# A hybrid decode step on one core: other slots for the pieces of the decode attention, and the first page gathers ahead of four memsets

## What is computed

```python
kc, vc = compress(rows[:, :, 0]), compress(rows[:, :, 1])   # every 16 tokens: an MLP over 32 tokens
o_cmp, p = cmp_attention(q, kc, vc)                         # softmax over 255 compressed keys
sel = top_k(select_blocks(p), 16)                           # 16 blocks of 64 tokens per kv head
o_slc = attention(q, k[sel], v[sel])                        # "chosen" keys and values
o_win = attention(q, window of the newest 512 tokens)       # "newest" keys and values
y = layernorm(alpha * x + (gated sum of all) @ w_out)
```

## Time and profile before

| | us |
|---|---|
| median of 3 runs (range) | 2114.49 (2113.04 to 2121.23) |
| the profiled execution's own time | 2107.58 |
| its span in the trace | 2105.8 |
| TensorE busy | 1971.9 (94%) |
| VectorE, ScalarE, GpSimd busy | 882.5, 735.3, 565.1 |
| loop of 384 slots, first product to the end of the last | about 1165.5 to 1839.2 |
| output projection, up to the last product | about 1839.2 to 2072 |

### The profile page before, as it was taken

How to read it: one execution, slowest core, us unless ns; L and a number is a source line. 1 busy time by engine, 2 the same in 40 slices (tenths; PEclk the granted TensorE clock), 3 DMA queues, 4 the chain that set the end, 5 groups by cost and what they waited for, 6 DMA issues and landing times. The chain is left out here.

```text
span 2105.8 us, 25188 instructions
## 1 busy us (share of the span) xinstructions
PE 1971.9 (94%) x9303; PEld 1356.8 (64%) x9303; DVE 882.5 (42%) x1781; ACT 735.3 (35%) x1345; POOL 565.1 (27%) x585
## 2 busy tenths in 40 slices
PE   8999999999999999999996898888888888899997
PEld 7888888888888887777774454444444444444442
DVE  0354545454531014444445355454554545511127
ACT  0231133213310003223323665666566665510013
POOL 0000000000002003343345476656466565030000
PEclk9999999999999999999998999999999999999999
DMA  5222222222222321111114555547374563563224
GB/s 199 89 80 91 91 71 80 91 91 71 80 82 102 100 95 48 61 41 41 41 41 140 170 160 171 168 156 218 107 211 143 176 214 111 196 241 142 80 80 161
DMA packets 76486, 248.95 MB, mean 118 GB/s; under 512 B 11764, under 2 KB 35520, under 8 KB 62176
## 3 DMA queue, kind: packets, MB, share of 16 engines
q1 hardware_dynamic: 46312, 148.04, 20.4%
q0 software_dynamic: 28800, 95.45, 15.0%
q10 hardware_dynamic: 1280, 4.23, 0.5%
HBM read 225.17 MB, written 22.49 MB: 118 GB/s over the span
## 5 line engine op out<-in xcount | busy, mean ns | idle before, releaser
L292 PE MATMUL pj<-xT,strips 128*128 128x260 f32 x2368 | 533.2, 384 | 6.3 <-DMA xT<-d_xT 6.3
L292 PEld LDWEIGHTS pj<-xT,strips 128*128 128x128 f32 x2368 | 446.4, 191 | 72.3 <-issue 6.2
L1869 ACT ACTIVATE big<-dtb 64x512 f32<-64x512 f32 x512 | 302.9, 592 | 164.0 <-PE dtb L1601 152.3
L792 PE MATMUL pj<-xT,strips 128*128 128x260 f32 x1216 | 291.0, 387 | 0.0
L1624 PE MATMUL dpH<-big,w 128*128 128x512 f32 x512 | 274.3, 621 | 0.9 <-DVE hs L1992 0.9
L792 PEld LDWEIGHTS pj<-xT,strips 128*128 128x128 f32 x1216 | 222.0, 190 | 59.1 <-issue 29.6
L1975 DVE TENSOR_TENSOR big<-big 128x512 f32<-128x512 f32 x128 | 88.1, 689 | 217.9 <-ACT big L1869 217.9
L1018 POOL MEMSET kbd<- 128x128 f32 x1 | 0.2, 204 | 635.9 <-POOLq L126 635.9
L1044 POOL TENSOR_SCALAR old<-old,rd 128x128 f32<-128x128 f32 (+3 forms) x116 | 122.0, 1066 | 166.8 <-DVE rd L1153 166.8
L1601 PEld LDWEIGHTS dtb<-const,xT 128*128 128x128 f32 x512 | 66.3, 150 | 127.8 <-issue 86.9
L1567 POOL DMA_INDIRECT KV<-d_cache,gi x104 | 102.4, 985 | 169.4 <-DVE gi L2111 140.1
(11 more groups left out here) (312 smaller groups left out, 2345.4 us busy)
## 6 DMA issues: line engine op xcount, KB each, us to landing
strips<-d_w_in SPq DMA_DIRECT2D x60, 1024.0 KB, 5.1
xT<-d_w_out SPq DMA_DIRECT2D x16, 1024.0 KB, 7.7
d_win_sample<-Wt SPq DMA_DIRECT2D x8, 1024.0 KB, 7.3
Xr<-d_w_out SPq DMA_DIRECT2D x8, 1024.0 KB, 8.6
Wt<-d_win SPq DMA_DIRECT2D x8, 896.0 KB
oT<-d_cache SPq DMA_DIRECT2D x84, 80.0 KB
xT<-d_xT SPq DMA_DIRECT2D x8, 520.0 KB, 9.8
Sold<-d_state SPq DMA_DIRECT2D x8, 512.0 KB, 5.2
```

Of the source, the lines that this page charges most:

```text
L292: mm = nc.tensor.matmul(pj[b][:, a, 0:TH], w[b][:, k, :], xT[:, k, a * TH:(a + 1) * TH], start=(k == 0), stop=(k == KT - 1))
L792: mm = nc.tensor.matmul(bank(s)[:, n, 0:TH], w[s % 2][:, k, :], xT[:, k, n * TH:(n + 1) * TH], start=(k == 0), stop=(k == KT - 1))
L1869: ins = A(dst[:, :, :, hd], tb[bank][hd * DH:(hd + 1) * DH].rearrange("p (j h n) -> p j h n", j=2, h=2), ACT.Copy)
```

## The change

New slots for 17 of the 36 entries of `AT` (`LAST` stays), and on GpSimd the first four gathers stand ahead of the memsets.

```diff
         AT = {
-            "queries": 19, ("second", 0): 27, ("second", 1): 29, "scores": 31, "weights": 35, "sums": 37,
-            "first": 38, "turned": 40, "values": 41, "slots": 42, "bases": 43, "rows": 48,
-            ("second", 2): 53, "fetch0": 54, ("second", 3): 55, "keys0": 58, "mix": 59, "fetch1": 61, "acc": 62,
-            "keys1": 64, "fetch2": 73, "keys2": 76, "fetch3": 80, "keys3": 82,
-            "SCORES": 87, "SCALE": 92, "TURNED": 94, "VALUES": 97, "NEWEST0": 99, "NEWEST1": 100,
-            "WSCORES": 105, "WSCALE": 108, "WTURNED": 111, "WVALUES": 113, "SUM": 114, "DONE": 118,
+            "queries": 19, ("second", 0): 26, ("second", 1): 29, "scores": 31, "weights": 35, "sums": 37,
+            "first": 38, "values": 41, "slots": 42, "bases": 43, "turned": 46, "rows": 48,
+            ("second", 2): 53, "fetch0": 54, ("second", 3): 56, "keys0": 57, "mix": 59, "fetch1": 61, "acc": 62,
+            "keys1": 63, "fetch2": 73, "keys2": 75, "fetch3": 78, "keys3": 81,
+            "SCORES": 87, "SCALE": 92, "NEWEST0": 93, "NEWEST1": 99, "TURNED": 100, "VALUES": 103,
+            "WSCORES": 106, "WSCALE": 108, "WTURNED": 112, "WVALUES": 114, "SUM": 117, "DONE": 124,
         }
@@ gpsimd
-            for n in range(2):
-                nc.gpsimd.memset(qbd[n][:], 0.0).then_inc(init, 1)
-            nc.gpsimd.memset(pn[:], 0.0).then_inc(init, 1)
-            nc.gpsimd.memset(sc[:], FORCED).then_inc(init, 1)
-
             def rows(b, q, par):
...
-            for q in range(4):
+            rows(0, 0, 0)
+            for n in range(2):
+                nc.gpsimd.memset(qbd[n][:], 0.0).then_inc(init, 1)
+            nc.gpsimd.memset(pn[:], 0.0).then_inc(init, 1)
+            nc.gpsimd.memset(sc[:], FORCED).then_inc(init, 1)
+            for q in range(1, 4):
                 rows(0, q, 0)
```

## The result

The changed kernel takes **2066.54 us** (median of 4 runs, 2063.09 to 2067.57) against 2113.76 (median of 4, 2111.83 to 2121.23) for the kernel before: ratio 0.9767, 95% interval 0.9741 to 0.9794. The forecast was 2083, with a range from 2067 to 2100.

A forecast was written before the change was run, and what follows sets the result against it. No engine was taken as full; TensorE, nearest, lost 12.8 us a sequence to waits and 2.6 to low clock. -37.2 - 1.0 + 7.1 - 0.4 = -31.5 gave 2076.1, plus 7 for the median: 2083 us, range 2067 to 2100.

The forecast's parts named there:

- the waits: TensorE's waits in each full sequence of the loop: 12.8 us before, 7.5 after, so 5.3 saved.
- the clock: Low stretches at 1.2 GHz in full sequences: 1.5 a sequence become one, at 1.7 us each, 0.9 us saved.
- The first sequence: The sequence before the six full ones has only the wait at `turned` and what lies behind it: -1.0 us.
- the tail: Loop's end: `mix` waits 9.3 us for a copy behind the residual's first addition, plus 2.2 of low clock: +7.1 us.
- the base: Profiled execution of the kernel before, 2107.6 us, lies 7 below the median of 2114.5, so 7 is added to 2076.1.
- slot 43: TensorE arrives earlier and waits for the first of ScalarE's eight emptyings (L1869): a new wait of 1.4 us.
- slot 48: Unit waits for bank 1, which VectorE empties only after differences, SCALE and the join (L2060): 1.7 us new.
- slots 24 to 26: Waits for the join and a bank, with SUM now between differences and join: 2.5 us in all.
- Rival 1: All low stretches in the loop go: -41.7 us, 2072.8 us; chance 0.17.
- After none of 2.0 to 2.3: In the kernel before's trace, no low clock stretch follows a TensorE wait of 2.0 to 2.3 us.
- Memsets: Phase start: the first four gathers, issued ahead of the memsets, shorten TensorE's first wait: -0.4 us, bounds 0 and 0.7.
- Rivals 2, 3 and 4: Waits return, 2105 us (0.13); chosen rows late, from 7 us over slower than 2125 (0.03); larger tail, 2088 (0.05).

The follow-up runs named there:

- all3: Changed kernel with (second, 3) in slot 55, VALUES 104, queries 17, SUM 115, and turned in slot 40 for sequence 0 alone; 2052.55 us, ratio 0.9705.
- scale_late_b: best_b with SCALE in slot 95 instead of 92; 2045.47 us, ratio 0.9649.
- second3: Changed kernel with (second, 3) in slot 55 and VALUES 104; 2060.45 us, ratio 0.9731.
- done_back: Changed kernel with DONE in slot 118, WVALUES 113 and SUM 114 again; 2077.16 us, ratio 0.98.
- chosen_only_b: Kernel before with only NEWEST0 in slot 93, NEWEST1 99, TURNED 100 and VALUES 104; 2091.8 us, ratio 0.9883.
- turned40: Changed kernel with turned back in slot 40 for every sequence; 2064.14 us, ratio 0.9744.
- x_tiles: Changed kernel with a semaphore for each of the four tiles of x; 2053.77 us, ratio 0.9692.
- best_b: all3 and x_tiles together; 2048.04 us, ratio 0.9663 (0.9459 on an odd chip).
- scores_early: all3 with SCORES in slot 84 instead of 87; 2060.39 us, ratio 0.9721.

## Why the prediction missed

**Two terms of the sum were mis-sized in the same direction, the waits (7.5 us a sequence forecast, 5.9 found) and the clock ("I take one a sequence", where one came in six).** In the profiles they make 10 and 6 us over the six sequences. The first sequence took 5 back, the tail gave 2: 13 us more than forecast, and the base, below, gave 3.5. The low end of the range had room for the clock term, since it holds no low stretch at all, but only for 0.5 us a sequence in the waits, where 1.6 came.

**The waits: 7.5 forecast, 5.9 found.** Every place was right, so the mechanism held, and six of the seven sizes were too high: slot 43 1.4 (1.26), slot 48 1.7 (1.36), WTURNED 0.3 (0.19), slots 24 to 26 2.5 (2.19), the second `second` 1.1 (0.83), keys3 0.4 (none); only the 0.1 before `sums` was 0.2. Added up over six sequences that is 10 us, more than the clock. Why the walk came out high nearly everywhere is not shown. That SUM ahead of the join costs 0.8 is shown by all3.

**The clock: one low stretch in six sequences, where six were forecast.** Rival 1 came true in the loop: all went but one. By the table the rest fell by 2.0 us a sequence against 0.9 forecast, 6 us in all. The place was not wrong: the one stretch stands right behind the two waits of slot 25, as feared. What failed is how often such waits cost a stretch. Waits of 1.4 us or less, single or in pairs, brought between none and five stretches in six sequences (scale_late_b, second3), so the forecast's six was more than any of these kernels shows. "After none of 2.0 to 2.3" did not carry over either: in done_back and chosen_only_b the 2.3 us wait did bring one. The Trainium skill's clock rule ("TensorE: Matmul & The Clock Gate", section "What's actually happening") had led to the right side here. The price of a stretch, 1.7, was too high by a quarter.

**First sequence: -1.0 forecast, +3.8 found.** The step "only the wait at `turned` and what lies behind it" left out the new wait at slot 48. Sequence 0 has no chosen scores yet, so nothing holds TensorE for 1.26 us at slot 43, and it reaches slot 48 3.1 us ahead of VectorE. The waits of that sequence rose from 6.1 to 7.1 us in all, and the other 2.8 us came with the 6.8 us of low clock behind the 3.1. With `turned` in slot 40 there, the first sequence is 71.2 (all3) and 71.9 us (turned40).

**Tail: +7.1 forecast, +5.5 found.** Mechanism and place were right (the copy behind the addition, `mix` behind the copy); 9.3 was 8.2. second3 gives 5.4 back by one slot, x_tiles shows that the wait for all four tiles was the root of it.

**Memsets: -0.4 forecast, nothing shown.** The first wait was 0.6 us shorter, of which 0.2 is left at the marker, and both are within the scatter of that wait. "Their issue moves from 1147.93 to about 1147.2" did not happen: the first gather starts 0.63 us behind VectorE's addition with nothing in front of it, where it was 0.73. It ends 3.1 us behind the addition's start in both kernels. That agrees with the rule that the prediction cites from "SBUF — State Buffer", section "Who interferes with whom", in the Trainium skill, by which the gather ends no earlier.

**The base.** I set the sum of 2076.1 off by 7 us because the profiled execution was 7 below its median. In the changed kernel the profiled execution is only 3.5 below its median: 2063.1 at a mean clock of 0.987, the other three 2066.2 to 2067.6 at 0.984 or 0.985, which is two to four stretches of 3.4 us. The kernel before scatters more: its seven executions beside best_b take 2109.69 to 2126.65 us, at mean clocks from 0.981 down to 0.974. So part of the offset of 7 probably went with the low stretches; how much isn't shown.

Rivals 2, 3 and 4 did not come: the waits for L2060 and L1869 stayed under 1.4, ScalarE never waits for `d_cache` rows in the six sequences, and the tail grew by less than forecast.

What stays open is why a 2.3 us wait brings a stretch in two kernels and not in the kernel before, where a stretch stood elsewhere in the sequence.

## What to carry over

When waits are rearranged, ask for each place where TensorE outruns another engine's chain how far ahead it gets in all: scores_early, turned40 and scale_late_b moved that time about without changing it, and only work taken out of the chain (SUM from in front of the join, a transfer that isn't waited for) shortened it. If it can't be removed, splitting it may help: with 1.3 + 1.4 us the profile of all3 has 3 us of low clock (second3 and x_tiles, split the same way, 17 and 14), with 2.7 in one place that of scores_early has 38 and 2 us more a sequence. And where an in-order engine will wait for a transfer, look at everything behind it, and wait for no more than the tile at hand.

## What I had not expected of the hardware

That kernels with equal waits differ so much in their clock: 38 and 3 us at 1.2 GHz in six sequences in the profiles of scores_early and best_b. That four 1 MB transfers issued together do not land together, though the DMA engines are full (share 1.01 from 1793 to 1821 us of x_tiles): the first was there 13.4 us before the last. And that a chip can differ by 7% from another in this kernel, for a reason that the traces don't show, and a change be worth 5.4% on it (best) that is worth 3.4% elsewhere.
